# Streaming encoder step: router logits from unnormalised rows, one-hots moved inside each expert, part of the last sum made earlier

## What is computed

```
h = x * rsqrt(mean(x*x) + EPS) * norm_ffn
p_group = softmax(h @ w_group_router)            # 4 groups, the best one
le = h @ w_expert_router                         # 16 logits, best 2 of the group's 4
gate = softmax(top 2 logits) * p_sel
for e in range(16):
    he = silu(h @ w_gate_e[e]) * (h @ w_up_e[e])
    out += dense_w[:, e] * (he @ w_down_e[e])
y = rmsnorm(x + out, norm_final)
```

## Time and profile before

| | us |
|---|---|
| median of 3 runs (lowest to highest) | 1280.15 (1276.65 to 1280.24) |
| profiled execution, its own time | 1275.22 |
| its span, first to last instruction | 1273.4 |
| PE, DVE, ACT busy | 1159.3, 721.1, 569.6 |
| mean granted TensorE clock | 0.954 of full |
| experts, from PE's first product to the last | 938.67 to 1248.8 |

### The profile page before, as it was taken

How to read it: one execution, slowest core, us unless ns; L and a number is a source line. 1 busy time by engine, 2 the same in 40 slices (tenths; PEclk the granted TensorE clock), 3 DMA queues, 4 the chain that set the end, 5 groups by cost and what they waited for, 6 DMA issues and landing times.

```text
span 1273.4 us, 18213 instructions
## 1 busy us (share of the span) xinstructions
PE 1159.3 (91%) x7804; PEld 1041.8 (82%) x7813; DVE 721.1 (57%) x832; ACT 569.6 (45%) x704; POOL 119.8 (9%) x131
## 2 busy tenths in 40 slices
PE   5998997999969999999899899789769999899995
PEld 4997687999957899999899899469747777778873
DVE  5312764664168843342434713633478998888884
ACT  4423562332247642222315523421156687677763
POOL 1000431000034200000000000000010110000031
PEclk9998887999979999999999999999869999999998
DMA  8432000231310133332526612000389999999996
GB/s 277 137 105 66 1 1 17 67 96 55 83 35 2 34 91 83 81 93 68 174 68 221 210 38 84 12 17 34 130 317 339 422 399 385 360 395 392 366 286 155
DMA packets 95004, 197.24 MB, mean 155 GB/s; under 512 B 4184, under 2 KB 71928, under 8 KB 82632
## 3 DMA queue, kind: packets, MB, share of 16 engines
q1 hardware_dynamic: 87328, 169.88, 38.3%
q0 software_dynamic: 5408, 18.76, 5.0%
q10 hardware_dynamic: 2184, 7.39, 1.4%
HBM read 178.41 MB, written 17.60 MB: 154 GB/s over the span
## 4 chain that ended last, share of the span: by engine, by line
PE 69%; DVE 20%; ACT 7%; issue 3%; DMA 1%; POOL 0%; SPq 0%; ACTq 0%; DVEq 0%; POOLq 0%
PE ps L1985 44%; DVE buf_r L847 9%; PE ps L909 6%; PE ps L919 2%; ACT buf_r L840 2%; PE ps L2352 1%; PE ps L2103 1%; DVE buf_r L1028 1%; PE ps L2104 1%; DMA buf<-in_w_in 1%; PE ps L2074 1%; PE ps L539 1%; DVE buf L577 1%; PE ps L893 1%; ACT buf_r L422 1%
## 5 line engine op out<-in xcount | busy, mean ns | idle before, releaser
L1985 PE MATMUL ps<-buf_r,buf_r 128*128 128x288 f32 (+1 forms) x4560 | 595.5, 292 | 12.8 <-DVE buf_r L438 9.7
L1985 PEld LDWEIGHTS ps<-buf_r,buf_r 128*128 128x128 f32 x4560 | 589.1, 190 | 14.7 <-issue 5.9
L428 DVE TENSOR_TENSOR buf_r<-buf,buf_r 128x2048 fp32r<-128x2048 f32 (+2 forms) x53 | 116.6, 2200 | 174.8 <-ACT buf_r L422 174.8
L847 DVE TENSOR_TENSOR buf_r<-buf,buf_r 128x2048 fp32r<-128x2048 f32 x96 | 213.9, 2283 | 0.0
L909 PE MATMUL ps<-buf_r,buf_r 128*128 128x512 f32 x768 | 187.7, 400 | 6.9 <-DVE buf_r L1028 6.9
L840 ACT CAST buf_r<-buf 128x2048 fp32r<-128x2048 f32 x96 | 178.8, 1908 | 12.8 <-DMA buf<-in_w_gate_e 11.3
L909 PEld LDWEIGHTS ps<-buf_r,buf_r 128*128 128x128 f32 x768 | 144.0, 191 | 38.3 <-DVE buf_r L1028 7.7
L422 ACT CAST buf_r<-buf 128x2048 fp32r<-128x2048 f32 (+2 forms) x53 | 96.6, 1823 | 117.2 <-PE ps L1985 65.9
L919 PE MATMUL ps<-buf_r,buf_r 128*128 128x512 f32 x384 | 92.4, 395 | 2.5 <-DVE buf_r L1052 1.4
L919 PEld LDWEIGHTS ps<-buf_r,buf_r 128*128 128x128 f32 x384 | 71.8, 188 | 20.4 <-DVE buf_r L847 2.4
L434 ACT CAST buf_r<-ps 128x1024 fp32r<-128x1024 f32 (+1 forms) x32 | 25.7, 802 | 75.4 <-PE ps L893 66.7
(11 more groups left out here) (313 smaller groups left out, 1208.6 us busy)
## 6 DMA issues: line engine op xcount, KB each, us to landing
buf<-in_w_gate_e SPq DMA_DIRECT2D x32, 1024.0 KB, 8.4
buf<-in_w_up_e SPq DMA_DIRECT2D x32, 1024.0 KB, 7.9
buf<-in_w_down_e SPq DMA_DIRECT2D x32, 1024.0 KB, 7.5
buf<-in_w_in SPq DMA_DIRECT2D x16, 1024.0 KB, 5.7
buf<-in_w_in SPq DMA_DIRECT2D x17, 512.0 KB, 4.7
buf<-in_w_mem_kv SPq DMA_DIRECT2D x8, 1024.0 KB, 5.7
y_rows<-buf ACTq DMA_DIRECT2D x14, 512.0 KB, 8.6
buf<-in_x_prompt SPq DMA_DIRECT2D x8, 512.0 KB, 5.3
```

The costliest lines, as they stand in the source:

```text
L428: nc.vector.tensor_tensor(r32(raw), raw, w_hi(n), ALU.subtract).then_inc(wl_ready, 1)
L847: nc.vector.tensor_tensor(e_lo(t), e_raw(t), e_hi(t), ALU.subtract).then_inc(wl_ready, 1)
L1985: last = nc.tensor.matmul(out, a, b, start=(k == 0 and j == 0), stop=(k == len(parts) - 1 and j == 2))
```

## The change

- Router: `HT` gets the turned rows of X itself. The gain goes into WR once, and the factor of each token is applied to its logits in `logits_out`. The scaled rows XNR are still made and stored, for the gather, but no step of the router waits for them. For the last chunk DVE now does the copy ahead of the scaling, and then the low part of tile 0.
- SP loads expert tiles 0 and 1 before the store of the last chunk's rows.
- After routing, DVE does the lows of tiles 1 and 2, the tokens of expert 0, then tile 3 (before: 0 to 3, then the tokens). ACT takes the tokens of expert 1 before tile 5.
- Groups are of two experts: seven of them, in experts 0 to 6. The one-hots stand between the product (line 1050) and the low part of the hidden rows (line 1052). `rows_step` is cut into four parts that stand at the same place in experts 8 to 11.
- In expert 15 PE makes `spread(0, 0)` before and `spread(1, 0)` after turning the hidden rows, then reads the count. ACT and DVE read the count ahead of the last result. That result is made in two halves, and `spread(0, 1)` waits for each half.

```diff
 def router_prepare(dve):
+    dve.wait_ge(wr_loaded, 96)
+    go(dve, nc.vector.tensor_tensor(WR, WR, bc(G_FFN.unsqueeze(2), [P, KD, 20]), ALU.mult))
 def logits_out(dve, m):
-    go(dve, nc.vector.tensor_copy(LG[:n, m, :], bank(3)[:n, 32 * m:32 * m + 20]))
+    dve.wait_ge(ri_ready, N_I + m + 1)
+    go(dve, nc.vector.tensor_scalar(LG[:n, m, :], bank(3)[:n, 32 * m:32 * m + 20],
+                                    RI[:n, N_I + m:N_I + m + 1], None, ALU.mult))
-GROUPS = ((3, 6), (6, 9), (9, 12), (12, 14), (14, 16))
+GROUPS = tuple((e, min(e + 2, NE)) for e in range(3, NE, 2))
+def spread(m, i, halves_=(0, 1), ready=None):
+    for h in halves_:
+        if ready:
+            nc.tensor.wait_ge(yol_ready, 2 + h)
...
+def spread_first(pe, m):
+    if m == 0:
+        pe.wait_ge(ht_ready, N_F + 3)
+        pe.wait_ge(yol_ready, 1)
+    spread(m, 0)
 def spread_pe(pe):
-    pe.wait_ge(ht_ready, N_F + 3)
-    pe.wait_ge(yol_ready, 1)
-    spread(0, 0)
-    spread(1, 0)
-    pe.wait_ge(yo_ready, NE)
-    pe.wait_ge(yol_ready, 2)
-    spread(0, 1).then_inc(sc_psum, 1)
+    spread(0, 1, ready=True).then_inc(sc_psum, 1)
     spread(1, 1).then_inc(sc_psum, 1)
 # SP
 for m, (t0, n) in enumerate(CH):
+    if m == NC_ - 1:
+        sp.wait_ge(mo_psum, 4 * NC_)
+        for t in range(2):
+            sp.dma_start(e_raw(t), E_TILES[t]).then_inc(mring_loaded[t], 16)
     sp.wait_ge(xn_ready, N_I + m + 1)
     sp.dma_start(hn_rows[t0:t0 + n, :], XNR[:n, m, :]).then_inc(hn_stored, 16)
 # PE, expert e
+    if e == NS_ + 1:
+        spread_first(pe, 0)
     pe.wait_ge(he_ready, e + 1)
 ...
     turn_hidden(HE).then_inc(het_psum, 1)
+    if e == NS_ + 1:
+        spread_first(pe, 1)
+        count = slots_needed(pe)
 # ACT
 silu(0)
+tokens_high(1)
 expert_high(act, 5)
 ...
+    if e == NE - 1:
+        count = slots_needed(act)
 ...
+    parts = ((0, D), ) if e == NS_ else ((0, HALF), (HALF, D))
 # DVE
-for t in range(4):
-    expert_low(dve, t)
+expert_low(dve, 1)
+expert_low(dve, 2)
 tokens_low(0)
+expert_low(dve, 3)
 gate_columns(dve)
 ...
     nc.vector.tensor_tensor(HE, bank(3), SG, ALU.mult).then_inc(he_ready, 1)
-    (the low part of the hidden rows)
     if e < len(GROUPS):
         group_one_hots(dve, e)
+    if 0 <= e - len(GROUPS) - 1 < 4:
+        rows_step(dve, e - len(GROUPS) - 1)
+    (the low part of the hidden rows)
     for i in range(1, 5):
         expert_low(dve, t + i)
-    if e == len(GROUPS) + 1:
-        rows_step(dve)
+count = slots_needed(dve)
 result_low(1)
 # DVE, last chunk before the experts
-ffn_scale(NC_ - 1)
 logits_out(dve, NC_ - 2)
 ffn_gain(NC_ - 1)
+ffn_scale(NC_ - 1)
+expert_low(dve, 0)
 # PE after the experts
-overflow(pe, overflow_pe, slots_needed(pe))
+overflow(pe, overflow_pe, count)
+with pe.If(count > P):
+    spread(0, 0)
+    spread(1, 0)
 # PE, memory output product of chunk m: its rows come from X, no wait for ffn_scale
-norm_turn(pe, N_I + m - 1, XNR[:n, m - 1, :], n, 4)
+turn_rows(m - 1)
+def turn_rows(m):
+    n = CH[m][1]
+    pe.wait_ge(x2_ready, 4 * (m + 1))
+    pe.wait_ge(ht_ready, N_I + m - 1)
+    for c in range(KD):
+        last = nc.tensor.transpose(norm_banks(N_I + m, 4)[:, c, 0:n], X[:n, m, c * P:(c + 1) * P], IDENT[:n, :n])
+    last.then_inc(tp_psum, 1)
```

More of the change, by code:

```diff
@@ L673, in group_out, with rows_step @@
             gates_out(dve, *GROUPS[g])
-        def rows_step(dve):
+        def rows_step(dve, part):
             v = nc.vector
[L678 to L692, removed]
@@ new lines, in rows_step @@
+            if part == 0:
+                go(dve, v.tensor_copy(POSP, bank(7)[:, 128:208].rearrange("p (c e) -> p c e", c=NC_)))
+                go(dve, v.tensor_copy(CNT, bank(7)[:, 208:224]))
+                go(dve, v.tensor_scalar(POSM, POSM, -1.0, None, ALU.add))
+                go(dve, v.tensor_scalar(TMP2, POSP, float(P), None, ALU.is_ge))
+                go(dve, v.tensor_reduce(FLAG[:, 0:1], CNT, AX.X, ALU.max))
+            elif part == 1:
+                for j in range(2, NC_):
+                    go(dve, v.scalar_tensor_tensor(out=TMP2, in0=POSP, scalar=float(P * j), in1=TMP2, op0=ALU.is_ge, op1=ALU.add))
+                go(dve, v.scalar_tensor_tensor(out=POSP, in0=TMP2, scalar=float((NE - 1) * P), in1=POSP, op0=ALU.mult, op1=ALU.add))
+                go(dve, v.tensor_tensor(POSP, POSP, bc(ECAP.unsqueeze(1), [P, NC_, NE]), ALU.add))
+            elif part == 2:
+                token_rows(dve, S1, R1F, 0)
+            else:
+                token_rows(dve, S2, R2F, 1)
+                v.tensor_copy(FLAG[:, 1:2].bitcast(U32), FLAG[:, 0:1]).then_inc(idx_ready, 1)
@@ L695, in router_scores, with token_rows @@
+        def token_rows(dve, s_, r, i):
+            v = nc.vector
+            go(dve, v.tensor_tensor(TMP, POSP, s_, ALU.mult))
+            go(dve, v.tensor_reduce(r, TMP, AX.X, ALU.add))
+            go(dve, v.scalar_tensor_tensor(out=R12[:, i, :].bitcast(U32), in0=r, scalar=NS_ * P + 0.5, in1=r, op0=ALU.is_lt, op1=ALU.mult))
+            go(dve, v.scalar_tensor_tensor(out=R12O[:, i, :].bitcast(U32), in0=r, scalar=NE * P + 0.5, in1=r, op0=ALU.is_gt, op1=ALU.mult))
         def router_scores(pe, m):
@@ L773, in encoder_step @@
         SC_BANK = (0, 2, 6, 4, 0)
[L775 removed]
+        HALF = D // 2
+        def spread(m, i, halves_=(0, 1), ready=None):
             t0, n = CH[m]
[L777 removed]
+            for h in halves_:
+                if ready:
+                    nc.tensor.wait_ge(yol_ready, 2 + h)
                 for y in (YOH[i], YOL[i]):
[L779 removed]
+                    last = nc.tensor.matmul(bank(SC_BANK[m] + h)[:n, :], r32(GMT[i][:, t0:t0 + n]), r32(y[:, HALF * h:HALF * (h + 1)]),
                                             start=(i == 0 and y is YOH[i]), stop=(i == 1 and y is YOL[i]))
             return last
[L783 to L791 removed]
+        def spread_first(pe, m):
[3 more added lines that the diff above has]
+            spread(m, 0)
+        def spread_pe(pe):
+            spread(0, 1, ready=True).then_inc(sc_psum, 1)
             spread(1, 1).then_inc(sc_psum, 1)
@@ L864, in experts_sp @@
             for m, (t0, n) in enumerate(CH):
+                if m == NC_ - 1:
+                    sp.wait_ge(mo_psum, 4 * NC_)
+                    for t in range(2):
+                        sp.dma_start(e_raw(t), E_TILES[t]).then_inc(mring_loaded[t], 16)
                 sp.wait_ge(xn_ready, N_I + m + 1)
                 sp.dma_start(hn_rows[t0:t0 + n, :], XNR[:n, m, :]).then_inc(hn_stored, 16)
-            sp.wait_ge(mo_psum, 4 * NC_)
-            for t in range(NT):
+            for t in range(2, NT):
                 if t == 4:
@@ L966, in experts_pe @@
                     turn_one_hots(pe, e - 11)
+            return count
         def experts_act(act):
@@ L1009, in experts_act @@
                 if e >= NS_:
-                    nc.scalar.activation(r32(YOH[e - NS_]), bank(5, 2), ACT.Copy, scale=GATE[:, e:e + 1]).then_inc(yo_ready, 1)
+                    parts = ((0, D), ) if e == NS_ else ((0, HALF), (HALF, D))
+                    for c0, c1 in parts:
+                        nc.scalar.activation(r32(YOH[e - NS_][:, c0:c1]), bank(5, 2)[:, c0:c1], ACT.Copy,
+                                             scale=GATE[:, e:e + 1]).then_inc(yo_ready, 1)
                     continue
@@ L1229, in moe_act @@
             act.wait_ge(idx_ready, 2)
-            experts_act(act)
+            count = experts_act(act)
             act.wait_ge(y_stored[0], 16 * (NS_ // 2))
-            overflow(act, overflow_act, slots_needed(act))
+            overflow(act, overflow_act, count)
             exp_and_ln()
@@ L1239, in moe_dve @@
             route_dve(dve)
-            experts_dve(dve)
-            count = slots_needed(dve)
+            count = experts_dve(dve)
             overflow(dve, overflow_dve, count)
@@ L1263, in moe_pe @@
             route_pe(pe)
[L1264 to L1265 removed]
+            count = experts_pe(pe)
+            overflow(pe, overflow_pe, count)
+            with pe.If(count > P):
+                spread(0, 0)
+                spread(1, 0)
             spread_pe(pe)
```

45 lines of the change are left out of this document (22 added, 23 removed).

## The result

The changed kernel took 1261.43 us in the median (1257.4 to 1263.51), beside 1278.4 for the kernel before. The ratio is 0.989, with an interval of 0.9855 to 0.9925. The forecast was 10.3 us, a ratio of 0.992, which lies inside both intervals; it is the traces, stage by stage, that show a gain of some 13 us. The range given, 1263.0 to 1275.5, misses the absolute median by 1.6 us; taken on the first median of 1280.15, the ratio gives 1266, inside it.

What follows compares the result with a forecast made beforehand. DVE was taken to bound the first experts, then a loop of PE, ACT and DVE. The terms 2.0 + 5.6 - 0.2 + 2.9 = 10.3 us led to a forecast median of 1269.5 us, range 1263.0 to 1275.5.

Steps and rivals of the forecast that it cites:

- What bounds: Whole kernel: DVE bounds the first experts, later a loop of PE, ACT and DVE in which PE hardly rests.
- Part A: Up to the first expert product: routing starts 1.5 us later, two lows fewer precede the tokens; 2.0 us earlier in sum.
- Each microsecond goes into the sum in full: Before routing: if tile 0 lands later than 5.5 us after its issue, each further microsecond is lost.
- Part B: Experts 0 to 7: one-hots fill DVE's 1.46 us wait, stretches with `group_out` become 19.1 us; 5.6 us earlier.
- The rival in which transfers bound: First experts stay as long because transfers bound them: Part B is 0, sum 4.7 us, time 1275.4; chance 0.06.
- Part C: Experts 8 to 15: PE keeps its work, four spread matmuls ahead of the turning in expert 15; 0.2 us later.
- Part D: After the last down product: halves and early spread products bring the first final addition 2.9 us earlier, ends 1.5 and 5.1.
- But the jump is still there: After the last down product: PE still waits for the jump and starts at about 1252.3, not free for the first half.
- I take most of the 3.66 as the jump's, not the reading's: PE's 3.66 us standstill after the last down product is mostly the jump's, since one 16 KB instruction packet is fetched there.
- The other branch of the forecast: If the reading costs, it stands ahead of the down product with only 0.4 us of cover; the end's gain is 2.5.
- the rival in which the fetch runs under the down product: At the end PE jumps at no cost, the count being known; sum 12.5 us, time 1267.3; chance 0.25.

Runs made afterwards that it cites:

- `no_router`: The changed kernel with the router part undone: scores from scaled rows, tiles 0 and 1 after the last store, lows 0 to 3 ahead of the tokens; ratio 0.991.
- `tiles_late`: The changed kernel with tiles 0 and 1 loaded after the last store again; first expert product 31.7 us after the last sum.
- `no_onehots`: The changed kernel with groups of three, one-hots and `rows_step` in their old places; ratio 0.9953.
- the late jumps: Changed kernel, PE reading the count early but jumping only when first half of the last low rows is ready; first final addition 11.1 us after the down product.
- experiment 5: The changed kernel with PE's count read behind the last down product (ratio 0.988), or its jump held for the last result's first half (first addition after 11.1 us).
- experiment 8: The changed kernel with tiles 0 and 1 loaded late, or tile 0's low part behind routing; first product 31.7 or 20.9 us after the last sum.
- `no_first`: The changed kernel with the eight early spread products behind the down product again, count still read early; first final addition 6.95 us after the down product.
- `changed_again`: The changed kernel itself, measured a second time beside a faster version; 1258.64 us, ratio to before 0.9883.
- `no_end`: The changed kernel without spread products in expert 15, counts read behind the last result, that result whole; ratio 0.9951.
- `whole_last`: The changed kernel with the last expert's result made whole; first final addition 4.07 us after the down product, against 3.32.

## Why the prediction was right, and where it was not

- **What bounds.** Right. DVE in the first experts, a loop of PE, ACT and DVE behind them. Stretches fell from 20.06 to 19.15 (19.1 forecast), beside the 18.4 of those without router work, which stayed.
- **Part A** (2.0 forecast, 3.1 measured against `no_router`: 0.5 ahead of the last sum, where 0.3 was forecast, and 2.6 behind it, where 1.7 was). The mechanism was as forecast: logits later against the last sum (1.2 us, 1.8 forecast), because they wait for tile 0, and two lows fewer ahead of the tokens. Tile 0 reached ACT 4.95 us after its issue, not 5.54, and this is 0.6 of the 0.9. "Each microsecond goes into the sum in full" was shown by `tiles_late`: 6.1 us later. I did not see that the order could be better.
- **Part B** (5.6 forecast, 5.1 in the traces, 5.1 to 5.5 against `no_onehots`). Right in size and in its steps: 3.2 for `rows_step`, 1.2 for the place, 0.5 to 1.2 for the smaller groups. The rival in which transfers bound fell.
- **Part C** (0.2 forecast). T(8) to T(15) is 0.2 longer, but only 0.1 of it is in expert 15 (15.29 to 15.37), where the forecast put it.
- **Part D** (2.9 forecast, 4.8 measured in the two first traces). This is the step that failed: "But the jump is still there", "I take most of the 3.66 as the jump's, not the reading's", and so PE would start some 3.5 us after the down product. It started after 1.97. That jumps cost was right, and 7.4 us for two is more than I gave them. Wrong was that their price stays behind the down product: the packet of the earlier trace rows, which began 1.0 us after that product, began 0.8 before its end, because the reading no longer stood ahead of it. I had put the reading at nothing; moving it back cost 3.3 us. The other branch of the forecast, in which an early reading would hold up the down product, fell too: PE's wait before that product is 0.47 us and ends with DVE's low part. I gave 0.25 to the rival in which the fetch runs under the down product, and that is nearly what happened, with 0.5 to 1.5 us left to wait. Its sum, 12.5, is close to what the stages give without chance, 0.5 + 2.6 + 5.1 - 0.2 + 4.8 = 12.8, but in part by luck: it has 1.1 too little in part A, 0.5 too much in part B and 0.3 too much in part D.
- **The rest of the 15.1 us.** 1.2 lie before the last sum, and 1.2 in the first products of the experts. The second is the clock's. The first is in code that the change leaves alone; that it is chance is likely and not shown. The last section says more.

The rule of the Trainium skill named in part D ("Runtime: NRT & Kernel Launch", Instruction fetch mechanics), that a taken branch to code outside the held pages stalls for a fetch, fits the 7.4 us of the late jumps and the one packet of instructions in them. The 108 ns for compare and branch of the Trainium skill ("Advanced Engine Details and Errata", Control Flow Timing) do not cover them. There is one such packet ahead of the first spread product, so one fetch, and by the two groups of experiment 5 the second jump adds only some 0.2 us behind it (2.8 to 2.9 for 2.6 to 2.7). What the 4.5 us ahead of the packet are, no run here shows.

## What to carry to other kernels

A register read and a branch cost little where the engine has work queued under which its sequencer can run ahead (0.5 to 1.5 us here), and several microseconds where the read itself stands behind that work: read early, and put the jump where enough products are still to run. A releaser named by the profile is checked against the time at which its data was ready: here the 0.5 us between them led to the jump. Before moving work under a wait, ask what the moved instruction waits for itself: a low part moved ahead of routing made routing wait for a transfer, and putting it back won 4.6 us. Where two engines take turns as the bound, look for the engine's own waits (here 1.46 and 1.2 us per expert) and fill them with its side work in pieces of that size.

## What the runs showed that I had not expected

**The same code reaches the same event up to 9 us apart.** Ten of the kernels profiled up to experiment 8 share all code ahead of the last sum (in `tiles_late` but for a transfer just before it). It lies between 900.3 and 909.1 us in them. A good part of it is in the stretch from 100 to 200 us. First the changed kernel, then `no_first`:

```profile
100.00:200.00 100.00, 88.08 (x469) 70.63 (x467) 59.64 (x53) 52.08 (x47) 29.68 (x43) 0.83 0.06 20
```

```profile
100.00:200.00 100.00, 87.84 (x507) 69.65 (x505) 62.53 (x56) 54.65 (x49) 30.86 (x44) 0.90 0.05 17
```

At a granted clock of 0.83 PE did 469 matmuls, at 0.90 it did 507. This code has many short gaps on PE, and how much of it runs at the lower clock differs between executions. The whole runs fit this: of the six of `changed_again` the fastest (1254.1 us) had a mean clock of 0.965 and the slowest (1264.4) one of 0.957. It is why stretches between common events tell more here than whole times.

**With a gap of PE filled its clock stayed up.** In `no_first` and `no_end` the last down product took 7.25 and 7.34 us with the clock at 0.50 at its start. In all eleven traces with spread products in the gaps it took 5.83 or 5.84. It was 5.84 in the kernel before too, so this is a risk taken away, not a gain in each execution.

**The clock gave and took the same.** The first 24 products of the experts took 7.16 us in the changed kernel's trace and 7.10 in `whole_last`, but 8.2 to 8.3 in the seven other traces of the same order: PE had been idle, and its clock rose to 1.00 earlier in the two. In the same two traces the memory output products up to the first turning took 19.0 us, and 17.5 in all others. So the 1.2 us won behind the last sum stand beside 1.5 lost ahead of it, and both come and go between traces of the same code.
